# A plain unit between the two shared units that a stage runs ahead for a down pair

## The reference

```
h = x + 0.5 * swiglu1(rms_norm(x))                 # D_FF = 5632
u = rms_norm(h)
q, k, v, f, gq, gk, gv, gr, gdown = split(u @ w_in)
A = forgetting_attention(q, k, v, log_sigmoid(f))  # 8 heads of 128
B = gated_linear_attention(gq, gk, gv, decay)      # 4 heads, chunks of 64
merged = sigmoid(gate_A) * (A @ W_A) + sigmoid(gate_B) * (B @ W_B)
h = h + merged @ w_out
h = h + 0.5 * swiglu2(rms_norm(h))
h = h + sigmoid(rms_norm(h) @ W_pg) * (p @ W_pe)
out = rms_norm(h)

swiglu(x) = (silu(x @ w_gate) * (x @ w_up)) @ w_down
```

## Time and profile before

| | us |
|---|---|
| median of 3 runs (2201.03 to 2201.58) | 2201.43 |
| the profiled execution | 2201.59 |
| its span, first to last instruction | 2199.9 |
| VectorE busy in it | 1592.3 |
| ScalarE busy in it | 1126.0 |

### The profile page before, as it was taken

How to read it: one execution, slowest core, us unless ns; L and a number is a source line. 1 busy time by engine, 2 the same in 40 slices (tenths; PEclk the granted TensorE clock), 3 DMA queues, 4 the chain that set the end, 5 groups by cost and what they waited for, 6 DMA issues and landing times.

```text
span 2199.9 us, 24417 instructions
## 1 busy us (share of the span) xinstructions
PE 2183.0 (99%) x9809; PEld 1798.9 (82%) x9809; DVE 1592.3 (72%) x1636; ACT 1126.0 (51%) x1187; POOL 40.4 (2%) x71
## 2 busy tenths in 40 slices
PE   9999999999999999999999999999999999999998
PEld 7888888888888888877777888888888888888786
DVE  5887889888887544445655665789878987888755
ACT  6554555554555544454444545455445555455554
POOL 0000000000000200010010000000000000000000
PEclk9999999999999999999999999999999999999999
DMA  8654655655554766665555665664565565556464
GB/s 306 220 182 174 244 189 178 217 186 203 196 209 140 211 191 193 178 180 168 173 171 161 183 190 182 221 215 158 210 229 179 191 222 184 205 200 202 137 216 144
DMA packets 146859, 425.68 MB, mean 194 GB/s; under 512 B 10664, under 2 KB 10672, under 8 KB 132288
## 3 DMA queue, kind: packets, MB, share of 16 engines
q1 hardware_dynamic: 144992, 419.21, 57.6%
q0 software_dynamic: 1472, 4.70, 0.7%
q10 hardware_dynamic: 288, 0.30, 0.0%
HBM read 422.06 MB, written 2.11 MB: 193 GB/s over the span
## 4 chain that ended last, share of the span: by engine, by line
PE 96%; DVE 2%; DMA 1%; ACT 1%; issue 1%; ACTq 0%; POOLq 0%; POOL 0%; DVEq 0%
PE acc L1577 11%; PE acc L1579 11%; PE acc L1578 11%; PE acc L1620 10%; PE acc L1622 10%; PE acc L1621 10%; PE turn L1620 5%; PE turn L1622 5%; PE turn L1621 5%; PE fox L1622 4%; PE fox L1621 4%; PE fox L1620 4%; PE turn L1597 1%; DVE w_lo L1153 0%; DMA raw<-in_ffn_up 0%
## 5 line engine op out<-in xcount | busy, mean ns | idle before, releaser
L1097 DVE TENSOR_TENSOR w_lo<-raw,w_hi 128x1024 fp32r<-128x1024 f32 x275 | 342.3, 1249 | 337.2 <-ACT w_hi L661 337.0
L661 ACT ACTIVATE w_hi<-raw 128x1024 fp32r<-128x1024 f32 x275 | 290.8, 1060 | 387.6 <-PE acc L1579 368.5
L1577 PE MATMUL acc<-w_hi,x_both 128*128 128x512 f32 x828 | 327.2, 395 | 1.7 <-DVE x_both L1272 1.7
L1579 PE MATMUL acc<-w_hi,x_both 128*128 128x512 f32 x828 | 322.7, 390 | 0.0
L1578 PE MATMUL acc<-w_lo,x_both 128*128 128x512 f32 x828 | 322.4, 389 | 0.0
L1577 PEld LDWEIGHTS acc<-w_hi,x_both 128*128 128x128 f32 x828 | 155.5, 188 | 39.4 <-issue 5.7
L1579 PEld LDWEIGHTS acc<-w_hi,x_both 128*128 128x128 f32 x828 | 155.4, 188 | 33.0
L1578 PEld LDWEIGHTS acc<-w_lo,x_both 128*128 128x128 f32 x828 | 155.6, 188 | 31.0
L718 ACT ACTIVATE w_hi<-raw 128x2048 fp32r<-128x2048 f32 x62 | 118.8, 1920 | 100.2 <-DVE more L1167 34.6
L718 ACT ACTIVATE more_r<-lo_raw 128x2048 fp32r<-128x2048 f32 x61 | 116.7, 1920 | 80.9 <-DVE more L1167 43.8
L1153 DVE TENSOR_TENSOR raw_r<-raw,w_hi 128x2048 fp32r<-128x2048 f32 x62 | 141.5, 2287 | 18.6 <-ACT w_hi L718 18.3
(11 more groups left out here) (497 smaller groups left out, 4957.0 us busy)
## 6 DMA issues: line engine op xcount, KB each, us to landing
raw<-in_w_in SPq DMA_DIRECT2D x96, 512.0 KB
lo_raw<-in_ffn_up SPq DMA_DIRECT2D x43, 1024.0 KB, 4.9
raw<-in_ffn_up SPq DMA_DIRECT2D x40, 1024.0 KB, 4.9
raw<-in_w_merge_gate SPq DMA_DIRECT2D x64, 512.0 KB
raw<-in_ffn_w_down SPq DMA_DIRECT2D x29, 1024.0 KB, 5.1
more<-in_ffn_up SPq DMA_DIRECT2D x28, 1024.0 KB, 4.9
lo_raw<-in_ffn_w_down SPq DMA_DIRECT2D x26, 1024.0 KB, 5.2
raw<-in_ffn_up SPq DMA_DIRECT2D x40, 512.0 KB, 3.8
```

The lines of the kernel that those rows point to most:

```text
L661: nc.scalar.activation(w_hi[:, slot, :, :], raw[:, slot, :, :], ACT.Copy).then_inc(hi_split, 1)
L1097: nc.vector.tensor_tensor(w_lo[:, slot, :, :], raw[:, slot, :, :], w_hi[:, slot, :, :].bitcast(F32), ALU.subtract).then_inc(lo_split, 1)
L1577: nc.tensor.matmul(to, hi(kt)[:, tok], w_hi[:, slot, k, :], start=kt == 0, stop=False)
L1579: last = nc.tensor.matmul(to, lo(kt)[:, tok], w_hi[:, slot, k, :], start=False, stop=kt == BK * nb - 1)
```

## The change

```diff
     own += plain
     if a:
-        own = [*own[:-1], *[("A", i + 1, u) for u in range(a)], own[-1]]
+        ahead = [("A", i + 1, u) for u in range(a)]
+        own = [*own[:-1], *ahead, own[-1]] if a > 2 else [*own[:-2], ahead[0], own[-2], ahead[1], own[-1]]
     return own
```

## The result

| | before | after |
|---|---|---|
| median (lowest to highest), us | 2201.58 (2200.93 to 2202.15), 13 runs | 2205.9 (2204.46 to 2209.19), 13 runs |
| ratio with its 95% interval | | 1.0021 (1.0013 to 1.0028) |
| profiled execution, us | 2201.59 | 2205.19 |
| span, us | 2199.9 | 2203.5 |
| mean granted clock of the span | 0.999 | 0.999 |

The kernel became slower by 4.3 us, or 0.2%: the interval excludes no change at all, and lies on both sides of the 0.2% that I had set as the line for "slower". The forecast for the median was 2205.0 us, measured are 2205.9; on which side of that line the kernel falls hung on 0.1 us. The profiled execution became 3.6 us longer, as forecast (2205.15, span 2203.5). The other 0.7 us of the median are not in that profile; they are the more instructive part.

The account below looks back on a forecast made before the run. TensorE, busy 2183.0 of 2199.9 us, was taken as the bound, so only its waits count: +2.40 +0.58 +0.58 = +3.56 us, profiled 2201.59 to 2205.15, median 2205.0 us; range 2200.9 to 2207.6.

Parts of the forecast that it names:

- Stages 15: Short stage in each FFN: old 1.11 us stall replaced by 1.69 us before the S item between A items; +0.58 us each.
- Stage 4 of the first FFN: S split behind A1's load-bound steps makes TensorE 2.25 us late, plus 0.15 us of slow first matmuls: +2.40 us.
- The estimate that stood beside it, 1.6 us: First FFN's stage 4: by the skill's DMA figure, 4.4 us for 1 MB, stall 1.6 instead of 2.4 us.
- The other stages ... at nothing: Three further down stages (least spare 2.6 us) and six up stages (least spare 0.8 us) were costed at 0.
- the least spare is 0.8 us: Six up stages before a down pair: VectorE's splits finish at least 0.8 us early, also the S split behind A1's steps.
- Rival (d): Gap of 2.25 us lets the clock fall for one S item, 5.44 us becoming 10.9: 2210.4 us; chance 0.03.
- 2.25 us is like 1.1 us: Argument against a clock fall in the first FFN's stage 4: earlier 1.1 us stalls left the clock at 1.00.
- Rival (a): Thin leads break at position 5 of six up stages and position 3 of stages 15: 2206.6 us or more; chance 0.17.
- The idle 1.00 us in the up stages: VectorE's idle time covers A0's moved steps, cost 0; if unusable, 0.11 + 0.15 us in each of six stages.
- Rival (b): Steps moved early remove both old TensorE waits and nothing new comes: -2.5 us, 2198.9 us; chance 0.06.
- Rival (c): Load of stage 4 lands earlier, shrinking the stall there under 1 us: 2201.4 to 2203.6 us; chance 0.08.

Follow-up runs that it names:

- e4: The kernel after, but VectorE splits the S item between the two A items before A1's steps; 2200.16 us, ratio 0.9993 to the kernel before.
- e8: The kernel after with the ring of load slots shifted so A1's load in stage 4 goes out one item earlier; 2202.66 us, ratio 1.0006 to the kernel before.
- e3: The kernel before with the new order only in nine stages, not stage 4 of the first FFN or the two stages 15; 2201.76 us, ratio 1.0001.
- e10: The kernel after run again without an edit, eleven executions; 2205.95 us against 2202.14 for the kernel before, ratio 1.0021.
- e11: The kernel after run again without an edit, one execution, to look at the clock behind the gap at 220 us; 2207.02 us.
- e12: The kernel after run once more without an edit, a second single execution for the same look at the clock; 2206.72 us.
- e5: The kernel before, item order kept, with A0's steps made one position earlier in the stages 15; 2199.17 us, ratio 0.9989.
- e9: The kernel after with idle VectorE additions before A1's steps in nine more stages, giving ten gaps of 2.18 to 2.92 us; 2239.8 us, ratio 1.0167 to the kernel before.
- e1: The kernel before with the new order only in stage 4 of the first FFN; 2204.27 us, ratio 1.0012.
- e6: The kernel before with the new order only in the first FFN's stage 4, plus two idle VectorE additions ahead of A1's steps there; 2209.07 us, ratio 1.0033.
- e7: The kernel before with the new order only in the first FFN's stage 4, plus four idle VectorE additions ahead of A1's steps there; 2210.76 us, ratio 1.0042.

## Why the prediction was right, and where it fell short

- **Stages 15, +0.58 each: right.** By the starts of the items the kernel falls back by 0.56 us in each. Every row of the working came out within 0.1 us (the S split ran from 674.61 in a kernel already 2.3 us later, against 672.31 forecast). The order of VectorE decides, as e4 shows.
- **Stage 4 of the first FFN, +2.40: right, with 2.50 measured.** Gap and slow first matmuls are there. The mechanism as told, a late load and a split queued behind it, stands by e4 and e8. What I took for granted held: A1's load is issued as before, since slots go by position, and lands within 0.13 us of it. The estimate that stood beside it, 1.6 us by the figure of the Trainium skill, did not come out. The section named there is on DMAs that GpSimd issues, and this load is two DMAs that SyncE issues.
- **"The other stages ... at nothing": wrong in one.** I took "the least spare is 0.8 us" for all six up stages, from A0's steps and from the splits where VectorE has its data. In stage 3 of the second FFN A1's steps wait for their load. In the trace of the kernel before they start at 1543.50 after 0.88 us of waiting, and the split behind them ends at 1548.44; the new due time is 1545.72 + 2.72 = 1548.44. Spare: 0, not 0.8. It cost 0.17 us in the profile of the kernel after and 0.65 in e3's. I had asked "bound by the load?" of the down stages alone. Timelines of VectorE and TensorE, kernel before:

```profile
1543.50 0.69 DVE L1164 TENSOR_TENSOR lo_raw<-lo_raw 128x512 f32<-128x512 f32 x1 [0.88 <-DMA room<-in_ffn_w_down]
1546.16 2.28 DVE L1153 TENSOR_TENSOR w_lo<-lo_raw,w_hi 128x2048 fp32r<-128x2048 f32 x1
...
1545.72 0.39 PE L1620 MATMUL turn<-w_hi,y_r 128*128 128x512 f32 x1
```

- **Rival (d), the clock: underrated and overpriced.** I gave it 0.03 and 5.4 us. It is in two of four profiles of the new kernel and costs 1.6 us, not the whole item at half rate: the clock came back before the item ended. So forecast and rival were not alternatives: they came together, in a part of the executions. That this is what lifts the median 0.7 us over the profiled execution is argued, not shown. In its favour: the means of the executions lie 4.5 us over those of the kernel before, in the result and in e10 alike, which is 0.7 more than the 3.79 us that the change costs in the profile without a fall, and a fall in half of the executions would give an estimate of 0.8. Against it: the medians of the same two kernels lie only 3.8 us apart in e10 (4.3 in the result), so they scatter by a few tenths anyway, and the start of the kernel has falls of its own (last section). The premise that failed is "2.25 us is like 1.1 us". "1.11 us and less" was also not the longest of the kernel before: at 12.47 us, next to the first stretch of the earlier trace rows, a matmul has waited 1.54 us, with a clock of 1.00 over the next 8 us. The new gap was still longer, and an unseen length deserved more than 0.03. The Trainium skill, "TensorE: Matmul & The Clock Gate", section "HAM oscillation — how this bites in real kernels", says that waits between bursts of matmuls can throttle the engine again. e11 and e12 agree, behind gaps shorter than the waits in that section's example.
- **Rival (a), thin leads: not seen** at position 5. The idle 1.00 us in the up stages was usable: e3's only new wait is the load-bound one above, behind A1's steps.
- **Rival (b), the early steps give the gain: half true.** They do, as e5 shows with -2.4 us (I had put -2.5). But the change gives the gain back in the same stage, by the S split behind A1's steps.
- **Rival (c):** the load landed where it had before.

## What to carry to other kernels

When two items change places on an in-order engine, list what is queued behind each of them, and compute its due time anew; ask of every such place separately whether a load is what it waits for. To bring preparation forward, move the preparation (e5), not the work around it: that kept both gains and cost nothing. A new gap on TensorE costs its length, and at times more than that, behind it.

## What the hardware showed that I had not expected

- Whether the granted clock falls behind one and the same gap of 2.0 to 2.9 us differs from execution to execution, and from gap to gap: two of four in the kernel after, eight of ten in e9, none of one in e1. Behind the gaps of 1.1 and 1.7 us in the stages 15 no profile showed it. When it falls, it does so after TensorE has resumed, about 1 us after the gap's end in e11 (0.78 over 221.0 to 221.5), and anywhere from at once to 2 us after it in e9, but within the longer gaps of e6 and e7.
- The kernel's start scatters too, in all versions. Over 10 to 20 us the granted clock was 1.00 in the profile of the kernel after, 0.83 in e10 and 0.66 in e3, whose profiled execution (2204.75) is 3 us above its median. Of that, 2.4 us come from the start (TensorE is 2.37 us behind the kernel before at 159 us) and most of the rest is the third wait. One stretch at the start explains more there than the change does; a single execution could not have told e3 from e1. Here e3:

```profile
10.00:20.00 10.00, 7.51 (x20) 5.94 (x21) 6.95 (x10) 6.97 (x13) 0.00 (x0) 0.66 1.03 395
```

- At the start too a gap is followed by a fall or not: TensorE has one wait that ends near 12 us. Behind one of 2.31 us (e10), 2.95 (e4) and 2.99 (e3) the clock fell; behind 2.65 (e8) and 3.02 (e7) it stayed at 1.00 over the next 8 us.
- How often the clock falls over many executions stays open: four profiles give no share.
